# Stick-breaking outputs made for a pair of heads at once instead of head by head

## The reference, cut to what matters

```python
def stick_breaking(q, k, v):
    scale = Dh ** -0.5
    for blk in range(L // SB_BLOCK):
        logits = einsum('bqhd,bkhd->bhqk', q[:, q0:kend], k[:, :kend]) * scale
        mask = ki < qi
        log_fail = where(mask, log_sigmoid(-logits), 0.0)
        between = cumsum(log_fail, axis=3, reverse=True) - log_fail
        w = where(mask, exp(log_sigmoid(logits) + between), 0.0)
        outs.append(einsum('bhqk,bkhd->bqhd', w, v[:, :kend]))
    return concatenate(outs, axis=1)
```

## Time and profile before

| | |
|---|---|
| median of 3 runs | 3117.12 us |
| the three runs | 3120.15, 3117.12, 3107.72 us |
| span of the profiled execution | 3111.0 us |
| TensorE matmul, busy | 2969.8 us (95%) |
| TensorE weight load, busy | 2412.7 us (78%) |
| VectorE, busy | 2122.5 us (68%) |
| ScalarE, busy | 1305.1 us (42%) |
| GpSimd, busy | 484.9 us (16%) |
| this stage, first transpose to last gate | about 124 us (2758.15 to 2882.07) |

### The profile page before, as it was taken

The page is one execution under the profiler, slowest core; times in us unless marked ns, Lnnn a source line. Parts: engine busy times, 40 slices in busy tenths (PEclk is TensorE's granted clock), DMA queues, the critical chain, the costliest instruction groups (busy, mean ns, idle before and its releaser), DMA issues. The chain is left out here.

```text
span 3111.0 us, 42087 instructions
## 1 busy us (share of the span) xinstructions
PE 2969.8 (95%) x14292; PEld 2412.7 (78%) x14292; DVE 2122.5 (68%) x3975; ACT 1305.1 (42%) x1965; POOL 484.9 (16%) x532
## 2 busy tenths in 40 slices
PE   7999999998989889999999999999998999999998
PEld 5678876887777777788888888888886777766787
DVE  5574434346888858888888888888894684446334
ACT  4443343332367752344444444444444432445222
POOL 1013442002466630000000000000001031024000
PEclk8999999999999999999999999999999999999999
DMA  2220002332234364443334334444432211200322
GB/s 107 75 68 22 28 25 72 112 115 88 89 119 171 138 220 134 139 135 119 119 126 135 126 120 131 135 135 135 129 121 76 88 48 61 82 27 1 122 95 88
DMA packets 138193, 316.99 MB, mean 102 GB/s; under 512 B 9296, under 2 KB 74960, under 8 KB 135888
## 3 DMA queue, kind: packets, MB, share of 16 engines
q1 hardware_dynamic: 133376, 280.33, 27.7%
q10 hardware_dynamic: 4688, 34.98, 2.7%
HBM read 275.43 MB, written 39.85 MB: 101 GB/s over the span
## 5 line engine op out<-in xcount | busy, mean ns | idle before, releaser
L205 DVE TENSOR_TENSOR split<-raw,split 128x1024 fp32r<-128x1024 f32 x172 | 209.9, 1226 | 407.8 <-ACT split L196 399.0
L196 ACT ACTIVATE split<-raw 128x1024 fp32r<-128x1024 f32 x216 | 227.0, 1057 | 602.8 <-PE proj L222 161.1
L2281 PE MATMUL up<-up_high,weight_high 128*128 128x512 f32 x700 | 272.3, 389 | 0.0
L2282 PE MATMUL up<-up_low,weight_high 128*128 128x512 f32 x700 | 272.3, 389 | 0.0
L2283 PE MATMUL up<-up_high,weight_low 128*128 128x512 f32 x700 | 272.3, 389 | 0.0
L373 POOL TENSOR_TENSOR xl<-col,xh 128x512 fp32r<-128x512 f32 x8 | 10.0, 1267 | 1072.7 <-ACT xh L345 1072.7
L1815 PEld LDWEIGHTS score<-hot,hot 128*128 128x128 f32 x1024 | 134.4, 199 | 44.5 <-issue 20.3
L1815 PE MATMUL score<-hot,hot 128*128 128x128 f32 x1024 | 140.6, 285 | 26.9 <-issue 14.6
L2410 PE MATMUL dt<-xh,split 128*128 128x512 f32 x416 | 161.9, 389 | 1.8 <-ACTq L2528 1.8
L2412 PE MATMUL dt<-xh,split 128*128 128x512 f32 x416 | 161.9, 389 | 0.0
L2411 PE MATMUL dt<-xl,split 128*128 128x512 f32 x416 | 161.9, 389 | 0.0
(11 more groups left out here) (548 smaller groups left out, 7863.5 us busy)
## 6 DMA issues: line engine op xcount, KB each, us to landing
raw<-in_stream SPq DMA_DIRECT2D x440, 512.0 KB, 3.6
gates<-stage ACTq DMA_DIRECT2D x16, 2048.0 KB, 6.5
gate<-gates SPq DMA_DIRECT2D x31, 1024.0 KB, 8.0
h<-in_x SPq DMA_DIRECT2D x4, 512.0 KB, 6.0
h<-in_x SPq DMA_DIRECT2D x1, 2048.0 KB, 8.0
h_saved<-h SPq DMA_DIRECT2D x1, 2048.0 KB, 7.5
h<-h_saved SPq DMA_DIRECT2D x1, 2048.0 KB, 13.3
rows<-h SPq DMA_DIRECT2D x4, 512.0 KB, 2.6
```

Of the source, the lines that this page charges most:

```text
L196: act.activation(g.high[t % slots], g.raw[:, t % RAW, :], ACT.Copy).then_inc(g.high_split, 1)
L205: dve.tensor_tensor(g.low[t % slots], g.raw[:, t % RAW, :], g.high[t % slots], ALU.subtract).then_inc(g.low_split, 1)
L2281: pe.matmul(bank, wh, uh, start=start, stop=False, skip_group_check=True)
L2282: pe.matmul(bank, wh, ul, start=False, stop=False, skip_group_check=True)
```

## The change

`output(u)` becomes `outputs(n)`, made once for a pair, after `sums` of an odd step. Its loop goes over the key blocks and within a block over the two heads, so that matmuls into partitions 0 to 63 and 64 to 127 take turns. An even step has no output on TensorE any more. As the even head's weights must now last until the odd head's are ready, a head has one of four buffers, shared by its soft logits and then its weights, in place of two and two. The memory taken is the same.

```diff
+HELD = 4
...
-        self.soft = [g.at(f"soft{s}", R + 54.5 + 2.5 * s, [P, WIDE]) for s in range(2)]
-        self.weight = [g.at(f"weight{s}", R + 59.5 + 2.5 * s, [P, WIDE]) for s in range(2)]
+        self.soft = [g.at(f"soft{s}", R + 54.5 + 2.5 * s, [P, WIDE]) for s in range(HELD)]
+        self.weight = [g.at(f"weight{s}", R + 54.5 + 2.5 * s, [P, WIDE]) for s in range(HELD)]
...
-        self.soft_lo = [g.at(f"soft_lo{s}", R + 54.5 + 2.5 * s, [P, WIDE], F32R) for s in range(2)]
+        self.soft_lo = [g.at(f"soft_lo{s}", R + 54.5 + 2.5 * s, [P, WIDE], F32R) for s in range(HELD)]
...
-        act.activation(self.b.weight[u % 2][:, :], self.lg[u % 2][:, 0:WIDE], ACT.Exp).then_inc(self.weighed, 1)
+        act.activation(self.b.weight[u % HELD][:, :], self.lg[u % 2][:, 0:WIDE], ACT.Exp).then_inc(self.weighed, 1)
...
-                def output(u):
-                    n, s = u // 2, u % 2
-                    pe.wait_ge(k.masked, u + 1)
-                    if s == 0:
-                        pe.wait_ge(v_read, n + 1)
-                        if n:
-
-                            pe.wait_ge(out_gated, n)
-                    half = slice(64 * s, 64 * s + 64)
+                def outputs(n):
+                    pe.wait_ge(k.masked, 2 * n + 2)
+                    pe.wait_ge(v_read, n + 1)
+                    if n:
+
+                        pe.wait_ge(out_gated, n)
                     for kb in range(TT):
-                        last = pe.matmul(ob[half, kb * P:], vr[:, kb, half], kb_of(weight[s], kb),
-                                         start=(kb == 0), stop=(kb == TT - 1), skip_group_check=True)
+                        for s in range(2):
+                            half = slice(64 * s, 64 * s + 64)
+                            last = pe.matmul(ob[half, kb * P:], vr[:, kb, half], kb_of(weight[(2 * n + s) % HELD], kb),
+                                             start=(kb == 0), stop=(kb == TT - 1), skip_group_check=True)
                     last.then_inc(out_made, 1)
...
-                    output(u)
-                    if u % 2 and u + 1 < SB_HEADS:
-                        turn_v(u // 2 + 1)
+                    if u % 2:
+                        outputs(u // 2)
+                        if u + 1 < SB_HEADS:
+                            turn_v(u // 2 + 1)
...
-                    dve.wait_ge(out_made, 2 * n + 2)
+                    dve.wait_ge(out_made, n + 1)
```

More of the change, by code:

```diff
@@ L3261, in sums @@
         s = u % 2
-        for half, ready in ((self.b.soft_hi, self.soft_high), (self.b.soft_lo[s], self.soft_low)):
+        for half, ready in ((self.b.soft_hi, self.soft_high), (self.b.soft_lo[u % HELD], self.soft_low)):
             pe.wait_ge(ready, u + 1)
@@ L3299, in mask_soft @@
         pool.wait_ge(self.softened, u + 1)
-        self.mask(pool, self.b.soft[u % 2], self.soft_masked)
+        self.mask(pool, self.b.soft[u % HELD], self.soft_masked)
     def mask_weight(self, pool, u):
         pool.wait_ge(self.weighed, u + 1)
-        self.mask(pool, self.b.weight[u % 2], self.masked)
+        self.mask(pool, self.b.weight[u % HELD], self.masked)
     def soften(self, dve, u):
@@ L3310, in soften @@
             dve.wait_ge(self.summed, u - 1)
-        dve.scalar_tensor_tensor(out=self.b.soft[u % 2][:, :], in0=self.lg[u % 2][:, 0:WIDE], scalar=0.0,
+        dve.scalar_tensor_tensor(out=self.b.soft[u % HELD][:, :], in0=self.lg[u % 2][:, 0:WIDE], scalar=0.0,
                                  in1=self.b.tmp[:, :], op0=ALU.max, op1=ALU.add).then_inc(self.softened, 1)
@@ L3319, in split_soft @@
             dve.wait_ge(self.summed, u)
-        soft, soft_hi = self.b.soft[u % 2], self.b.soft_hi
+        soft, soft_hi = self.b.soft[u % HELD], self.b.soft_hi
         dve.tensor_copy(soft_hi[:, :], soft[:, :]).then_inc(self.soft_high, 1)
         dve.wait_ge(self.soft_high, u + 1)
-        dve.tensor_tensor(self.b.soft_lo[u % 2][:, :], soft[:, :], soft_hi[:, :],
+        dve.tensor_tensor(self.b.soft_lo[u % HELD][:, :], soft[:, :], soft_hi[:, :],
                           ALU.subtract).then_inc(self.soft_low, 1)
```

## The result

The median after the change is 3134.86 us (six runs, 3123.76 to 3142.10) against 3115.28 us for the kernel before (six runs, 3107.72 to 3120.15). The ratio is 1.0061, 95% interval 1.0044 to 1.0078. The forecast of 3119.6 us (3109 to 3129) was wrong: the change costs some 20 us, more than the 0.5% that a measurement can tell.

A forecast was written before the change was run, and what follows sets the result against it. TensorE was taken as the bound, with a ring of waits through ScalarE only some 0.6 us a step behind. Terms −1.7 − 2.6 + 6.8 = +2.5 us, put on the median, gave 3119.6 us (3109 to 3129).

The forecast's parts named there:

- the ring: Chain of waits from one head's logits through ScalarE's softplus and `weigh` to the next logits: at least 7.50 us a step.
- Step 1: Odd step, now with both heads' outputs: 8.46 us against 8.16, +0.30, including 0.2 us of waiting for rounded halves.
- The pair's outputs: Both heads' output matmuls side by side in the odd step: 2.40 us, between bounds of 2.30 and 4.60.
- The gap: TensorE idle at the end of each even step, before the logits, waiting for `weigh`: 2.17 us.
- step 7, the masks: Pair's outputs wait only for the odd head's mask from GpSimd: covered by 0.8 us, no cost.
- step 6, the gap and the clock: Six new TensorE gaps of 2.17 us bring four clock falls, about 1.7 us each: +6.8 us.
- step 3: Six pairs of steps, even step −0.58 and odd step +0.30 each: −1.7 us.
- a rival and a chance of 0.06: Clock stays at half for 6.6 us after each of six gaps: +16.1 us, 3133.2 us; chance 0.06.
- step 4, the start: Stage start, where step 0 loses its output at the slow clock: −2.6 us.
- step 5, the end: Stage end: last pair starts when head 15's output did and takes some 0.1 us more; counted as nothing.
- a kernel without falls: Rival: the clock stays at full after the six gaps, −4.3 us, 3112.8 us; chance 0.27.
- The skill's rules: Rival from strict program order: only neighbouring products overlap, 0.46 us more per pair, +3.2 on the forecast, 3122.8 us; chance 0.08.

The follow-up runs named there:

- split version: Changed kernel with each pair's output products split over the odd and the next even step, the gate one step later: 3103.66 us, run again 3102.15 us.
- kernel with nine fillers: Changed kernel plus nine useless 512-column matmuls at the end of each of six even steps: 3110.66 us, ratio 0.9991.
- kernel with four fillers: Changed kernel plus four useless matmuls at the end of each of six even steps, leaving gaps of 1.2 us: 3115.07 us, ratio 1.0005.
- without turns: Changed kernel with the pair's products split over two steps and, within each part, the even head's products before the odd head's: 3097.20 us, ratio 0.9957.
- dense fillers behind it: Changed kernel plus eight useless 512-column matmuls after the gap, ahead of the odd step's logits, the gap left as it is: 3131.57 us, ratio 1.0059.

## Why the prediction was wrong

**Right, by its own steps.** The bound by the ring: even step 7.50 forecast, 7.48 measured, and the split version's pair of 14.98 is twice that. Step 1, the odd step at full clock: 8.46 forecast, 8.47 in the kernel with nine fillers; here two small errors cancel, waits of 0.3 us for the halves instead of 0.2 and outputs of 2.30 instead of 2.40. The pair's outputs: 2.40 forecast; 16 instructions last 2.38 us, 2.30 to the next start, the lower bound. The gap: 2.17 forecast, 2.16 measured, put down to ScalarE's `weigh`. The halves do run side by side, and step 7, the masks, held inside the pairs.

**Wrong: step 6, the gap and the clock.** The mechanism was named and even said to decide the sign, but its term was mis-sized twice. Four falls were taken, there were six. The reading of the rows was wrong here: 2.17 us does not lie between the gap without a fall (2.18) and the one with (2.34) but below both, so by length alone the rows spoke for no fall. And length alone does not decide, as the equal waits with and without a fall show. Each was priced at 1.7 us, from a fall that was followed by dense 512-column matmuls; here each costs 4.5 us of the odd step, because the logits follow and the clock stays down for 10 us instead of 3.4. Forecast 4 × 1.7 = 6.8 us, measured 6 × 4.5 = 27 in the profiled execution; with the −1.7 of step 3 that is the 25.2 us of the six pairs. The row that was nearer in kind was at hand: at this stage's own start the same sort of work had kept the clock down for 6.6 us. I gave it a rival and a chance of 0.06, with a price of 3.4 us a gap. That its 3133.2 us is the result to 2 us is partly luck: its change of +16.1 us stands against 19.6 between the medians and 26.4 in the profiled execution.

**Wrong in size: step 4, the start.** 2.6 us forecast, 1.2 measured. With its output gone, the stretch at half clock after the barrier is 10 us long instead of 6.8, so the sums run slowly throughout. It is the same mistake. The kernel with four fillers has the same program at this place, but its low stretch began 0.9 us into the logits and was 6.8 us long; there the start took 11.9 us against 14.75 before, a gain of 2.8, near the forecast. Its busy time:

```profile
2763.30:2769.80 6.50, 6.50 (x21) 0.50 0.00 0
```

**Wrong in size: step 5, the end.** Nothing was forecast. Within the stage it came out as nothing, but by two changes that cancel. The last head's sums no longer wait 1.78 us for VectorE, as the slow odd step before them gives it time. The last pair, after a wait of 2.52 us for head 15's mask on GpSimd, runs at half clock, 4.54 us against 4.04 for both heads before and 2.38 for a pair at full clock. The low stretch begins in that wait and reaches into the next stage, which accounts for the 2.6 us behind it. The kernel with nine fillers, without falls in the pairs, shows the price in the stage itself. Its last pair:

```profile
2874.52 4.06 PE L3517 MATMUL attn<-weight,v_rows 128*64 128x512 f32 x16 [2.52 <-POOL weight L3297]
```

It takes 4.06 us instead of 2.38, and the stage 123.2 us against 124.75, a gain of 1.6 where 4.3 was forecast for a kernel without falls. Of the missing 2.7 us, half is lost at the start, where the gain is 1.25 and not 2.6, and half after the last transposes, where this pair at half clock costs 1.7.

**The skill's rules.** By the Trainium skill's page "TensorE: Matmul & The Clock Gate", section "Part 3: Packing small matmuls — row/col tiling", matmuls start and end strictly in program order. The runs don't agree: two products a head, of 512 and 384 columns, take 1.73 us for both heads without turns, about what one head's two take alone (2.30 × 896 / 1280 = 1.6 us to the next start). The page "TensorEngine Tiling (Array Packing)", section "Key Properties", says that different tiles can load weights and multiply in parallel, independently of each other. With that the trace agrees, as long as no more than three instructions of the first half are waiting to start.

## What to carry to other kernels

When TensorE is the busiest engine by a small margin, moving its work together can open a gap elsewhere, and the gap may be paid in clock, not in idle time: here 2.16 us of waiting cost 4.5 us more of work. Price it by what TensorE does right after the gap, from a row with the same kind of work, not by the gap's length, and look whether the same saving can be spread so that no step has a gap at all, as splitting the pair did. A useless matmul in a gap is a cheap test of whether the clock is the cause.

## What the runs showed of the hardware

- Matmuls into the two partition halves of a PSUM bank run fully side by side in fp32: 16 instructions in 2.38 us, where 8 of one half alone take 2.37. They need no turns in the program when four instructions of one half stand ahead (1.73 us against 1.72), and do when eight do (3.93 us).
- In this stage a TensorE gap of 1.63 us before 64-row logits brought the clock down six times of six, one of 1.17 us three times of six. With dense fillers behind it, a gap of 2.16 us did so four times of six. A wait of 2.66 us before the last sums had a fall in one run of the split kernel and none in the other. The length of the gap doesn't decide alone.
- With the split and turns, where no wait for `weigh` is above 0.8 us, one run had no fall inside the pairs and the other had one.
- A stretch at half clock inside the pairs lasted 3.4 us (sums or dense 128-row fillers in it), 6.8 (part of the logits) or 10.2 (all of them, or nearly).
- Fifty-four useless matmuls made the program 24 us faster.
